# Preparing the next block's input later in the middle rounds of a fused sequence-mixing and expert kernel

## The reference

```
h    = rmsnorm(x) * (1 + scale1) + shift1
proj = h @ W_in                                  # 1024 -> 3072: conv value, conv gate, q, f, i, g
conv = silu(layernorm(depthwise_conv31(val * sigmoid(gate))))
rec  = HGRN2(q, f, i) in chunks of 64, per-head rmsnorm, * silu(g)     # 4 heads of 128
x    = x + gate1 * rmsnorm(concat(conv, rec) @ W_out)
h    = rmsnorm(x) * (1 + scale2) + shift2
x    = x + gate2 * rmsnorm(two_of_32_experts(h))   # best group of 8, then two experts in it
```

## Time and profile before

| | us |
|---|---|
| median of 3 runs | 1662.14 (1656.52 to 1665.27) |
| profiled execution | 1662.17, span 1660.4 |
| TensorE busy | 1520.1 (92% of the span) |
| VectorE busy | 1210.6 (73%) |
| ScalarE busy | 876.0 (53%) |
| GpSimd busy | 367.1 (22%) |
| mean granted TensorE clock | 0.954 of full speed |

### The profile page before, as it was taken

The page is one execution under the profiler, slowest core; times in us unless marked ns, Lnnn a source line. Parts: engine busy times, 40 slices in busy tenths (PEclk is TensorE's granted clock), DMA queues, the critical chain, the costliest instruction groups (busy, mean ns, idle before and its releaser), DMA issues. The chain is left out here.

```text
span 1660.4 us, 23932 instructions
## 1 busy us (share of the span) xinstructions
PE 1520.1 (92%) x7453; PEld 1106.6 (67%) x7455; DVE 1210.6 (73%) x1932; ACT 876.0 (53%) x1534; POOL 367.1 (22%) x396
## 2 busy tenths in 40 slices
PE   4899879999989999999999999658999999999974
PEld 2779754889755889666889565445676677766741
DVE  2587994597975598974698945576788878777837
ACT  3324362324574324563324533356788887878846
POOL 1000000000010000011000011123476667665640
PEclk8899979999999999999999998769999999999996
DMA  9452361332332323332321543469999998889859
GB/s 320 168 185 94 93 260 42 89 102 78 126 102 76 102 79 100 116 113 77 89 89 52 228 127 114 153 228 329 352 295 274 344 262 240 223 243 284 275 109 384
DMA packets 201445, 291.27 MB, mean 175 GB/s; under 512 B 10558, under 2 KB 158171, under 8 KB 201370
## 3 DMA queue, kind: packets, MB, share of 16 engines
q1 hardware_dynamic: 171840, 197.18, 34.8%
q0 software_dynamic: 29360, 92.99, 20.5%
q10 hardware_dynamic: 170, 0.10, 0.0%
HBM read 240.42 MB, written 59.26 MB: 180 GB/s over the span
## 5 line engine op out<-in xcount | busy, mean ns | idle before, releaser
L1038 DVE SCALAR_TENSOR_TENSOR cv<-late_rows,taps,cv 128x512 f32<-128x512 f32 x480 | 321.8, 746 | 0.0
L1962 DVE TENSOR_TENSOR w_rest<-wgu,w_high 128x1024 fp32r<-128x1024 f32 x192 | 233.8, 1221 | 88.9 <-ACT w_high L1885 85.5
L1885 ACT ACTIVATE w_high<-wgu 128x1024 fp32r x192 | 201.7, 1054 | 97.9 <-PE pgu L1830 75.9
L531 PE MATMUL bank<-wo,yT 128*128 128x512 f32 x512 | 226.5, 599 | 3.6 <-ACT hT L736 2.5
L488 PE MATMUL bank<-hT_high,tiles_operand 128*128 128x512 f32 x496 | 197.2, 398 | 1.1 <-DVE logits L1132 1.1
L489 PE MATMUL bank<-hT_operand,tiles_operand 128*128 128x512 f32 x496 | 196.6, 396 | 0.0
L490 PE MATMUL bank<-hT_high,win_operand 128*128 128x512 f32 x496 | 196.6, 396 | 0.0
L531 PEld LDWEIGHTS bank<-wo,yT 128*128 128x128 f32 x512 | 96.7, 192 | 119.7 <-issue 117.7
L1840 PE MATMUL py<-wd,hTe 128*128 x384 | 172.7, 592 | 1.8 <-DVE hTe L1985 0.9
L1828 PE MATMUL pgu<-w_high,x_high 128*128 128x512 f32 x384 | 156.8, 408 | 3.8 <-DVE x_rest L1977 3.8
L1016 DVE TENSOR_TENSOR win_operand<-win,tiles_operand 128x2048 fp32r<-128x2048 f32 x48 | 109.9, 2290 | 58.1 <-ACT tiles_operand L758 58.0
(11 more groups left out here) (389 smaller groups left out, 2846.7 us busy)
## 6 DMA issues: line engine op xcount, KB each, us to landing
win<-w_in_in SPq DMA_DIRECT2D x64, 512.0 KB, 5.2
wgu<-w_gate_in SPq DMA_DIRECT2D x32, 1024.0 KB
wgu<-w_up_in SPq DMA_DIRECT2D x32, 1024.0 KB
wd<-w_down_in SPq DMA_DIRECT2D x32, 1024.0 KB
win<-w_in_in SPq DMA_DIRECT2D x16, 1024.0 KB, 5.1
wo<-w_ada_in POOLq DMA_DIRECT2D x6, 2048.0 KB, 11.2
y_dram<-zeros POOLq DMA_DIRECT2D x17, 512.0 KB, 5.1
tiles<-x_in POOLq DMA_DIRECT2D x16, 512.0 KB, 6.0
```

The costliest lines, as they stand in the source:

```text
L531: last = nc.tensor.matmul(out[:], yT[:, w % 2, k, :], wo[:, k, half * 512:(half + 1) * 512], start=(k == 0), stop=(k == KD - 1))
L1038: ins = V.scalar_tensor_tensor(out=cv[:, j], in0=u[:, j, w:w + T], scalar=tap, in1=cv[:, j], op0=ALU.mult, op1=ALU.add)
L1885: A(w_high[:, QK * q:QK * q + QK, :], c.wgu[:, bass.ds(slot, 1), QK * q:QK * q + QK, :].rearrange("p a k n -> p (a k) n"), ACT.Copy).then_ ...
L1962: V.tensor_tensor(w_rest[:, part, :], c.wgu[:, bass.ds(slot, 1), part, :].rearrange("p a k n -> p (a k) n"), w_high[:, part, :].bitcast(F3 ...
```

## The change

In the middle rounds (blocks 1 and 2):

- On TensorE T(0) to T(3) go from among the first two y and the mean to behind O(1), B(2), O(2) and B(3); y(1,1) is issued in two parts of four matmuls, around B(0); r and oT move a little at the end.
- On ScalarE and VectorE xsum, xnorm, raw, high and input follow them to later places, and some entries near them change places.
- In these rounds T(1) and T(3) use banks 0 and 1, T(0) and T(2) banks 2 and 3.

For all rounds the square in xsum writes its full-size output, which nobody reads, to hT in place of ob; with that osave no longer waits for x_rstd, and modulate (raw on VectorE) waits for its tile's.

```diff
             if kind == "T":
-                return 2 * (1 if i == 3 else i) + half if t < 0 else 2 + half
+                return 2 * (1 if i == 3 else i) + half if t < 0 else 2 + half if t == 0 or i % 2 == 0 else half
...
-            def y_half(t, w, half):
-                if half == 0:
+            def y_half(t, w, half, part=None):
+                first, final = part in (None, 0), part in (None, 1)
+                if half == 0 and first:
...
-                out = take("y", w, half, t)
-                for k in range(KD):
+                out = take("y", w, half, t) if first else place("y", w, half, t)
+                for k in range(0 if first else KD // 2, KD if final else KD // 2):
...
-                last.then_inc(y_ready, 1)
+                if final:
+                    last.then_inc(y_ready, 1)
...
-            MIDDLE = [("y", 0, 0), ("T", 0), ("mean",), ("T", 1), ("y", 0, 1), ("T", 2), ("var",), ("T", 3), ("y", 1, 0),
+            MIDDLE = [("y", 0, 0), ("mean",), ("y", 0, 1), ("var",), ("y", 1, 0), ("A", 0), ("y", 1, 1, 0), ("B", 0),
+                      ("y", 1, 1, 1), ("O", 0), ("A", 1), ("r", 0), ("B", 1), ("l", 0), ("O", 1), ("T", 0), ("A", 2),
+                      ("oT", 0), ("B", 2), ("T", 1), ("r", 1), ("l", 1), ("y", 2, 0), ("oT", 1), ("O", 2), ("T", 2),
...
-                if i == 0:
-                    wait(act, oT_psum, (t - 1) * NT)
                 act.wait_ge(*x_landed(t, i))
-                ch.link(A(ob[:].rearrange("p a n -> p (a n)"), xt_of(t, i), ACT.Square, accum_out=sums[:, i:i + 1]))
+                ch.link(A(hT[:, :, i * P:(i + 1) * P], xt_of(t, i).rearrange("p (k n) -> p k n", k=KD), ACT.Square,
+                          accum_out=sums[:, i:i + 1]))
...
             def modulate(t, i):
 
+                dve.wait_ge(x_rstd, t * NT + i + 1)
                 out = place("T", i, 1, t - 1)
...
-                elif t < NB - 1:
-                    dve.wait_ge(x_rstd, (t + 2) * NT)
                 else:
-                    dve.wait_ge(oT_psum, t * NT)
+                    wait(dve, oT_psum, t * NT)
```

More of the change, by code:

```diff
@@ L915, in _ @@
                      ("turned", 3)]
[L916 to L923, removed]
+            MIDDLE = [("ln", 0), ("ln", 1), ("ln", 2), ("end", 0), ("exps", 0), ("sq", 0), ("sq", 1), ("sq", 2),
+                      ("sq", 3), ("exps", 1), ("end", 1), ("ln", 3), ("exps", 2), ("end", 2), ("var",), ("ysum", 0),
+                      ("exps", 3), ("end", 3), ("xsum", 0), ("gate",), ("key", 0), ("x1sum", 0), ("xsum", 1),
+                      ("ysum", 1), ("key", 1), ("rin", 0), ("osq", 0), ("orstd", 0), ("x1sum", 1), ("raw", 0),
+                      ("key", 2), ("turned", 0), ("osq", 1), ("raw", 1), ("rin", 1), ("orstd", 1), ("high", 0),
+                      ("turned", 1), ("high", 1), ("xsum", 2), ("split", 0), ("ysum", 2), ("raw", 2), ("x1sum", 2),
+                      ("xsum", 3), ("osq", 2), ("high", 2), ("orstd", 2), ("key", 3), ("ysum", 3), ("raw", 3),
+                      ("x1sum", 3), ("rin", 2), ("high", 3), ("osq", 3), ("rin", 3), ("orstd", 3), ("turned", 2),
+                      ("split", 1), ("turned", 3)]
             FINAL = [("ln", 0), ("ln", 1), ("ln", 2), ("end", 0), ("exps", 0), ("sq", 0), ("sq", 1), ("sq", 2), ("sq", 3),
@@ L1204, in _ @@
                      ("gateo", 2), ("oms", 3), ("gateo", 3), ("rest", 1), ("logit", 3)]
[L1205 to L1215, removed]
@@ new lines, in _ @@
+            MIDDLE = [("scan", 0), ("diff", 0), ("centre",), ("head", 0), ("scan", 1), ("diff", 1), ("scan", 2),
+                      ("head", 1), ("diff", 2), ("scan", 3), ("head", 2), ("diff", 3), ("scale",), ("head", 3),
+                      ("ynorm", 0), ("mask", 0), ("state", 0, 0), ("place", 0), ("x1norm", 0), ("xnorm", 0),
+                      ("state", 0, 1), ("ynorm", 1), ("mask", 1), ("osave", 0), ("xnorm", 1), ("state", 1, 0),
+                      ("oms", 0), ("gateo", 0), ("state", 1, 1), ("logit", 0), ("osave", 1), ("x1norm", 1),
+                      ("raw", 0), ("mask", 2), ("state", 2, 0), ("oms", 1), ("raw", 1), ("place", 1), ("gateo", 1),
+                      ("logit", 1), ("input", 0), ("state", 2, 1), ("xnorm", 2), ("osave", 2), ("input", 1),
+                      ("raw", 2), ("ynorm", 2), ("rest", 0), ("oms", 2), ("x1norm", 2), ("input", 2), ("xnorm", 3),
+                      ("mask", 3), ("gateo", 2), ("place", 2), ("ynorm", 3), ("state", 3, 0), ("raw", 3),
+                      ("x1norm", 3), ("osave", 3), ("state", 3, 1), ("oms", 3), ("logit", 2), ("input", 3),
+                      ("gateo", 3), ("logit", 3), ("place", 3), ("rest", 1)]
```

## The result

| | before | changed |
|---|---|---|
| median | 1661.10 us (1656.52 to 1665.27) | 1698.54 us (1697.02 to 1699.20) |
| ratio, 95% interval | | 1.0225 (1.0208 to 1.0242) |
| profiled execution | 1662.17, span 1660.4 | 1698.32, span 1696.1 |
| round of block 1 | 110.96 | 129.48 |
| round of block 2 | 109.42 | 124.87 |

The change makes the kernel 37.4 us slower. The forecast was 1689 (27 us slower) with a range of 1676 to 1698, so the side was right and the size too small by 10 us. The round lengths of the table go from the first y to the second projection group; the windows shown with the earlier trace rows begin and end up to 0.1 us beside these points.

What follows compares the result with a forecast made beforehand. TensorE, busy for 92% of the span, was taken as the bound, so its waits count. Profiled 1662.2 us + 23.0 of waits (11.5 per middle round) + 4.2 of clock = 1689.4, said as 1689, range 1676 to 1698.

Steps and rivals of the forecast that it cites:

- A(0): TensorE, first half of a middle round: a new wait because it stands one y half earlier; about 1.4 us.
- O(1): TensorE, first half: waits for state(1,0), in front of which VectorE now has xnorm(1); 1.0 us.
- B(2): TensorE, first half: now directly behind oT(0), waits for turned(0); 0.8 us.
- l(1): TensorE, first half: now directly behind r(1), waits while ScalarE does raw(1) and rin(1); 1.2 us.
- T(2): TensorE, second half: waits for xnorm(2), whose xsum(2) stands behind turned(1) and high(1) on ScalarE; 2.2 us.
- y(3,0): TensorE, second half: waits for raw(2), behind ysum(2) on ScalarE, which wants the end of y(2,1); 3.2 us.
- O(3): TensorE, second half: waits for state(3,0), now behind ynorm(3) on VectorE; 3.4 us, before 0.28.
- the projection group: TensorE, end of a middle round: first projection group waits for input(3), behind logit(2) on VectorE; 1.5 us, before 0.38.
- oT(2): TensorE, second half: waits for state(3,1), which comes after O(3), with r(2) covering half; 0.9 us.
- What was taken at nothing: Cut of y(1,1), banks for odd tiles, square to hT, modulate's wait: some 0.1 us each; moved DMAs hidden.
- the clock term: TensorE's clock in the two middle rounds: about four falls in place of one, +4.2 us, bounded by -1.4 and +12.6.
- Rival 2: Middle rounds: many waits keep the clock falling, behind most of them; 1662.2 + 23.0 + 12.6 = 1698 us; 20%.

Runs made afterwards that it cites:

- e1_raw_first: The changed kernel with raw(2) moved ahead of ysum(2) on ScalarE in the middle rounds; 1689.91 us, ratio 1.0156.
- e3_fill: The changed kernel with unread matmuls added on TensorE in each middle round, 2 before T(2), 3 before y(3,0), 3 before O(3); 1693.89 us, ratio 1.0187.
- e9_fill_more: The changed kernel with 12 unread matmuls added per middle round, ahead of seven of TensorE's waits; 1687.53 us, ratio 1.0155.
- e2_state_first: The changed kernel with state(3,0) moved ahead of ynorm(3) on VectorE in the middle rounds; 1704.32 us, ratio 1.0263.
- e4_scratch_only: The kernel before with only the square's output in hT, the wait in modulate, and osave not waiting for x_rstd; 1662.67 us, ratio 1.0001.
- e5_banks_back: The changed kernel with T(1) and T(3) put back on banks 2 and 3, new orders kept; 1694.51 us, ratio 1.0203.

## Why the prediction was wrong

**The waits were right.** Worked out and measured, in us per round: A(0) 1.4 and 1.50; O(1) 1.0 and 1.0; B(2) 0.8 and 0.87; oT(0) 1.0 and 0.78; l(1) 1.2 and 1.26; B(0) and A(1) together 0.7 and 0.42; T(2) 2.2 and 2.19; y(3,0) 3.2 and 3.21; O(3) 3.4 and 3.39; the projection group 1.5 and 1.47; oT(2) 0.9 and 0.22 or none in the changed kernel, where the clock had slowed r(2) ahead of it (0.92 where it had not, in e1_raw_first and e3_fill). Idle time grew by 10.6 and 10.4 us where 11.5 were forecast. With the clock up (e9_fill_more) the rounds are 11.5 us longer each than the 109.4 of one without a fall, as worked out. Moving one entry removes y(3,0)'s wait (e1_raw_first), and e2_state_first shows that O(3)'s is not that of one entry.

**What was taken at nothing cost nothing** as far as it was tested: the square, the wait in modulate and osave's (e4_scratch_only). The piece of W_in behind T(3) was never waited for: the projection has no idle time. The cut of y(1,1) in two parts has no run of its own.

**The failing step is the clock term.** The prediction put it at "about four falls in the two rounds in place of one, +4.2 us", at 1.4 us each. Measured, the rounds are 34.0 us longer together. Of these 23.0 are the waits at the length that they have with the clock up (e9_fill_more), the term that was worked out; the other 11.0 are the clock's, in place of 4.2. A further 1.7 us stand outside the two rounds. Seen from TensorE, 21.0 of the 34.0 us are new idle time and 13.0 are the same matmuls taking longer, and filling the waits takes 12.5 us away.

Two errors are in the term. The count: the prediction gave falls to waits of over 2 us alone, but the clock also fell at O(1)'s 1.0 and l(1)'s 1.26, which stand among small matmuls; there are seven falls in place of one, six more and not three. The trace of before could have told: its one fall stands at the 1.3 us in front of O(0), which the prediction lists but doesn't connect with it.

```profile
475.00:480.00 5.00, 3.49 (x31) 2.58 (x29) 1.48 (x4) 2.52 (x7) 0.02 (x1) 1.00 0.26 105
480.00:485.00 5.00, 4.53 (x32) 4.16 (x33) 2.04 (x7) 2.31 (x8) 1.70 (x2) 0.66 0.40 134
```

The price: the 1.4 us came from windows of which the second began a little early and ended a little late; between the exact points the two rounds of before differ by 1.5. The six more falls cost 1.8 us each, since two of the seven lasted twice as long; a fall at a long wait cost 1.8 on the y behind it (8.80 against 7.03).

Rival 2 (+12.6 us, 1698) is the case that came, and its mechanism, falls at most of the long waits, is nearer to the trace than the forecast's. That its time is met within 1 us is partly luck: it has nine more falls at 1.4 us, where six more were measured at 1.8, and the 1.7 us outside the rounds make up the difference. The Trainium skill's section on psum-queue depth-cycling ("TensorE: Matmul & The Clock Gate") stood beside that rival: short idle times between groups of matmuls make the clock go back and forth, at a cost between the bursts. The trace of the changed kernel agrees in part: seven falls in two rounds with 12 and 11 waits, so not one at each, and at waits for results of other engines as well as for a bank. The prediction's count of six such waits per round of before is five, of 0.69 to 1.30 us, beside some of under 0.4.

**What stays open.** Which waits bring a fall is not settled: 4.6 us lie between the two rounds of the changed kernel, whose waits are alike, and T(2)'s 2.2 us brought one in the second round alone, y(3,0)'s 3.2 in the first alone. And the 5 to 6 us between the two forms of block 3's round, which is the same program in all runs, are in every median here; the difference of 37.4 us is free of it as far as the two profiles go (743.7 and 742.5 from that round's start), that of e5_banks_back is not.

## What to carry to other kernels

When work is moved in an order written by hand, look on each engine at what now stands directly ahead of each entry, and ask whether that waits for the instruction group just ahead of the one which will need the result; such a pair costs its whole chain of durations, and it can be read from the orders and the old durations without a run. A wait at the end of a chain is removed only by other work that can run there: swapping its last link moves it. Price the clock beside the waits: in this kernel 21.0 us of new idle time brought 13.0 us of slower matmuls, some 60% on top, and the waits that brought falls were as short as 1.0 us. A single wait of 4.63 us cost 1.8 on top. These ratios are from this kernel alone; in another, fill the waits with matmuls that nobody reads, and see what the time does.

## What was not expected of the hardware

- Matmuls whose result nobody reads make the kernel faster: 12 per round took 12.5 us off the two rounds (120.9 in place of 129.5 and 124.9), since the granted clock stays at 1.00.
- The clock fell at waits of 1.0 and 1.26 us among small matmuls, not only at those of over 2 us; a single wait of 4.63 us among dense ones brought a fall in both rounds.
- A round of the same program (block 3's, up to its last logits) takes 143.6 to 143.9 us in three profiles and 147.9 to 150.9 in the other eight. Some 100 us into it the clock stays at its lower level for about 3 us in the three, and for about 10 or more in the others.
